# Second layer with three projection banks, a head's softmax beside the output projection, and reordered loads

## What is computed

```python
def dilated_mixer(h, w_in, w_out):
    q, k, v, z = jnp.split(h @ w_in, 4, axis=-1)            # 16 heads of 128
    q = rotary(q, pos) * (B_HEAD_DIM ** -0.5)
    k = rotary(k, pos)
    for window, dilation in B_CONFIGS:                      # (128,1), (512,4), (2048,16)
        o_g, lse_g = _dilated_band_attention(q, k, v, window, dilation)
    alpha = jax.nn.softmax(jnp.stack(lses), axis=0)
    o = jnp.einsum('gbsh,gbshd->bshd', alpha, jnp.stack(outs))
    return (o * jax.nn.silu(z)) @ w_out

def reference(x, norm_g, final_g, ...):
    h = x
    for layer in range(DEPTH):                              # DEPTH = 2
        u = rmsnorm(h, norm_g[layer])
        h = h + mixer(u, w_in, w_out)                       # dsa_mixer, then dilated_mixer
    return rmsnorm(h, final_g)
```

## Time and profile before

| | |
|---|---|
| median of 3 runs | 967.16 us (965.05 to 967.76) |
| the profiled execution | 967.73 us; its span, first to last instruction, 964.9 us |
| PE busy | 936.3 us, 97% of the span, 4603 matmuls |
| DVE / POOL / ACT busy | 647.5 (67%) / 563.4 (58%) / 443.2 us (46%) |
| mean granted clock of the matmul engine | 0.994 of full |
| chain that ended last | PE 76%, DVE 17%, issue 3%, POOL 2%, DMA 1%, ACT 1% |
| HBM read | 78.52 MB, 84 GB/s over the span |

### The profile page before, as it was taken

One profiled execution on the slowest core, in us unless ns is written; L12 is line 12 of the kernel. 1 busy time (PEld: TensorE's weight loads), 2 busy tenths in 40 slices (PEclk: granted clock), 3 DMA queues, 4 the chain that ended last, 5 costly groups with the idle time before them and its releaser, 6 DMA issues.

```text
span 964.9 us, 12633 instructions
## 1 busy us (share of the span) xinstructions
PE 936.3 (97%) x4603; PEld 790.9 (82%) x4603; DVE 647.5 (67%) x1241; ACT 443.2 (46%) x770; POOL 563.4 (58%) x395
## 2 busy tenths in 40 slices
PE   6999999999999999999899999999999999999996
PEld 5898888888888888878688888888888888878886
DVE  4798798665665644467776776666677677654456
ACT  6565323544544632355344554454445445442323
POOL 2875444555555444476666666667676676654445
PEclk9999999999999999999999999999999999999998
DMA  8422223121121122312222222221222212213212
GB/s 301 151 88 83 93 88 107 47 66 44 45 66 44 44 88 91 106 66 88 69 84 81 73 88 88 66 88 66 88 80 73 87 66 88 88 44 96 101 66 87
DMA packets 25133, 81.43 MB, mean 84 GB/s; under 512 B 2928, under 2 KB 5232, under 8 KB 25072
## 3 DMA queue, kind: packets, MB, share of 16 engines
q1 hardware_dynamic: 23920, 79.57, 24.8%
q10 hardware_dynamic: 1152, 1.06, 0.3%
HBM read 78.52 MB, written 2.10 MB: 84 GB/s over the span
## 4 chain that ended last, share of the span: by engine, by line
PE 76%; DVE 17%; issue 3%; POOL 2%; DMA 1%; ACT 1%; SPq 0%; POOLq 0%; DVEq 0%; ACTq 0%
PE ps L312 14%; PE ps L314 13%; PE ps L313 13%; DVE bias_a L1007 11%; PE ps L422 6%; PE ps L421 6%; PE ps L420 6%; DVE by_sin L927 2%; PE ps L371 2%; PE ps L372 2%; PE ps L370 2%; PE ps L385 2%; DMA w_raw<-weights 1%; PE ps L412 1%; PE ps L411 1%
## 5 line engine op out<-in xcount | busy, mean ns | idle before, releaser
L1205 POOL TENSOR_TENSOR w_lo<-w_raw,w_hi 128x1024 fp32r<-128x1024 f32 x137 | 338.2, 2469 | 301.9 <-ACT w_hi L581 301.3
L312 PE MATMUL ps<-u_hi,w_hi 128*128 128x512 f32 (+1 forms) x856 | 337.2, 394 | 17.6 <-DVE u_lo L870 8.3
L314 PE MATMUL ps<-u_hi,w_lo 128*128 128x512 f32 (+1 forms) x856 | 331.7, 388 | 0.0
L313 PE MATMUL ps<-u_lo,w_hi 128*128 128x512 f32 (+1 forms) x856 | 331.3, 387 | 0.0
L581 ACT ACTIVATE w_hi<-w_raw 128x1024 fp32r<-128x1024 f32 x138 | 146.0, 1058 | 217.4 <-PE ps L314 112.2
L312 PEld LDWEIGHTS ps<-u_hi,w_hi 128*128 128x128 f32 x856 | 161.6, 189 | 54.4 <-DVE by_cos L928 13.4
L314 PEld LDWEIGHTS ps<-u_hi,w_lo 128*128 128x128 f32 x856 | 161.4, 189 | 31.8
L313 PEld LDWEIGHTS ps<-u_lo,w_hi 128*128 128x128 f32 x856 | 161.8, 189 | 29.7 <-issue 0.5
L1007 DVE STREAM_TRANSPOSE bias_a<-probs 32x320 f32<-32x320 f32 x240 | 120.6, 502 | 4.7 <-POOL probs L1248 1.6
L1248 POOL TENSOR_SCALAR probs<-probs,inv_den 128x512 f32<-128x512 f32 (+3 forms) x128 | 66.1, 540 | 48.6 <-DVE inv_den L996 48.6
L660 ACT ACTIVATE probs<-neg_s,neg_max 128x512 f32<-128x512 f32 (+3 forms) x128 | 70.6, 554 | 23.4 <-DVE neg_max L989 23.2
(11 more groups left out here) (149 smaller groups left out, 1541.4 us busy)
## 6 DMA issues: line engine op xcount, KB each, us to landing
w_raw<-weights SPq DMA_DIRECT2D x138, 512.0 KB, 3.2
gated<-x_rows SPq DMA_DIRECT2D x4, 512.0 KB, 8.0
h<-x_turned SPq DMA_DIRECT2D x7, 256.0 KB, 7.4
outT<-h SPq DMA_DIRECT2D x10, 128.0 KB, 1.9
outT<-h ACTq DMA_DIRECT2D x6, 128.0 KB, 2.2
w_raw<-weights SPq DMA_DIRECT2D x2, 256.0 KB, 5.4
table<-rope_tables SPq DMA_DIRECT2D x2, 256.0 KB, 7.0
table<-rope_tables SPq DMA_DIRECT2D x1, 512.0 KB, 6.4
```

The lines of the kernel that those rows point to most:

```text
L312: pe.matmul(out, w_hi[:, g % SLOTS, blk], u_hi[:, k, tokens], start=(at == 0), stop=False)
L313: pe.matmul(out, w_hi[:, g % SLOTS, blk], u_lo[:, k, tokens], start=False, stop=False)
L314: last = pe.matmul(out, w_lo[:, g % SLOTS, blk], u_hi[:, k, tokens], start=False, stop=(at == KT - 1))
L1205: pool.tensor_tensor(w_lo[:, g % SLOTS, :], w_raw[:, g % 2, :], w_hi[:, g % SLOTS, :].bitcast(F32), ALU.subtract).then_inc(w_lo_ready, 1)
```

## The change

- `BANK`: the projections of the second layer go through banks 0, 1 and 7 in turn.
- `head_b`: head hd's gate is projected in the same iteration, behind its V. VectorE reads the gate's bank behind V's, no longer ahead of the transposes. On ScalarE the silu and the load back to Exp move behind the rounding of K and of the next tile, directly ahead of `v_part`. ScalarE and POOL split their four weight tiles one tile later in the list. In iteration 15 only two steps of the gate's projection stand ahead of the output of head 14, then `last_head`.
- `last_head` (PE): scores, turn of V, six steps of the gate's projection; then blocks 2, 3 and 4 of row 0 of the output projection, `turn_probs`, block 1, `output`. `out_projection(1, 0)` leaves these four blocks out. On the other engines the last head's work is the second branch of iteration 15; there is no iteration 16.
- First layer: the first two steps of query 3 are taken ahead of `turn_probs(0)`.
- Start: SP issues tiles 2 and 3 ahead of the half table, then the identity, then all rows; ScalarE squares the rows behind the rounding of tile 3.

The diff, with little context:

```diff
@@ -51,7 +51,7 @@
-BANK[N_B + 3] = 7
+BANK[N_B:] = [(0, 1, 7)[i % 3] for i in range(4 * HEADS)]
@@ -71,6 +71,8 @@
 S_BANK, T_BANK = 2, 5
+FREE_BLOCKS = (2, 3, 4)
+BEGUN_BLOCKS = FREE_BLOCKS + (1,)
@@ -244,15 +246,13 @@
                 sp.dma_start(h[:, m, :], xT[m * P:(m + 1) * P, :]).then_inc(x_landed[m], 16)
+            load_tile(2)
+            load_tile(3)
             sp.dma_start(table[0:P // 2, 2:4, :], rope_tables[0:P // 2, 2:4, :]).then_inc(key_table_landed, 16)
-            load_rows(0)
-            load_tile(2)
-            load_rows(1)
-            load_tile(3)
-            load_rows(2)
-            load_rows(3)
             sp.dma_start(ident[:, :], ident_in).then_inc(ident_landed, 16)
+            for i in range(QB):
+                load_rows(i)
@@ -428,6 +428,8 @@
                 for m in M_ORDER:
+                    if layer and t == 0 and m in BEGUN_BLOCKS:
+                        continue
@@ -464,13 +466,16 @@
                 if query:
-                    project(G_Q[hd], range(0, KT // 2))
+                    project(G_Q[hd], range(2 if hd == 3 else 0, KT // 2))
                     output(hd - 3)
                     project(G_Q[hd], range(KT // 2, end))
+                if hd == 2:
+                    project(G_Q[hd + 1], range(0, 2))
@@ -486,32 +491,31 @@
             def head_b(hd):
-                new, last_new = hd < HEADS, hd == HEADS - 1
                 n, tile = HEADS + hd - 1, G_B + 4 * hd
-                if new:
-                    scores(n, 0, R_B + 2 * hd - 1)
-                    if hd > 1:
-                        project(tile - 1)
-                    project(tile)
-                    project(tile + 1)
-                    project(tile + 2, range(0, 5 if last_new else KT))
-                    if hd == 1:
-                        pe.wait_ge(bank_read[7], 1)
-                    output_by_parts(n)
-                else:
-                    project(tile - 1, range(0, 2))
-                    turn_v(tile - 2)
-                    project(tile - 1, range(2, 6))
-                    pe.wait_ge(v_lo_ready, HEADS + 1)
-                    turn_probs(n)
-                    project(tile - 1, range(6, KT))
-                    output(n)
-                if last_new:
-                    scores(n + 1, 0, R_B + 2 * hd + 1)
-                    project(tile + 2, range(5, KT))
-                if new and not last_new:
+                scores(n, 0, R_B + 2 * hd - 1)
+                for g in range(tile, tile + 3):
+                    project(g)
+                project(tile + 3, range(0, 2 if hd == HEADS - 1 else KT))
+                output_by_parts(n)
+                if hd < HEADS - 1:
                     turn_v(tile + 2)
+            def last_head():
+                n, tile = 2 * HEADS - 1, G_OUT[1]
+                scores(n, 0, R_B + 2 * HEADS - 1)
+                turn_v(tile - 2)
+                project(tile - 1, range(2, KT))
+                wait_for_head(1, 0)
+                for m in FREE_BLOCKS:
+                    out_block(1, 0, m, ALL, True, False)
+                pe.wait_ge(v_lo_ready, HEADS + 1)
+                pe.wait_ge(bank_read[7], BANK.count(7))
+                turn_probs(n)
+                pe.wait_ge(bank_read[1], BANK.count(1))
+                out_block(1, 0, 1, ALL, True, False)
+                output(n)
@@ -560,8 +564,9 @@
             first_head_b()
-            for hd in range(1, HEADS + 1):
+            for hd in range(1, HEADS):
                 head_b(hd)
+            last_head()
@@ -695,32 +700,26 @@
             def head_b(hd):
-                new, attend, last_new = hd < HEADS, hd > 0, hd == HEADS - 1
                 n, tile, r = HEADS + hd - 1, G_B + 4 * hd, R_B + 2 * hd
-                if attend:
-                    split_w(tile + 1)
-                if not new:
-                    v_part(hd)
-                    split_o(1, 0)
-                if attend and new:
+                if hd:
                     split_w(tile + 2)
-                    silu(n, hd - 1, tile - 1)
+                    split_w(tile + 3)
+                    turned_hi(n)
+                rope_hi(r, q_hi[:, 0, :])
+                split_w(tile + 4)
+                rope_hi(r + 1, k_hi[:, :])
+                split_w(tile + 5)
+                if hd < HEADS - 1:
+                    silu(n + 1, hd, tile + 3)
                     act.preload_act_table(ACT.Exp)
-                    split_w(tile + 3)
-                if attend and new:
-                    turned_hi(n)
-                if not new:
-                    probs_hi(n)
-                    silu(n, hd - 1, tile - 1)
-                if new:
-                    rope_hi(r, q_hi[:, 0, :])
-                    split_w(tile + 4)
-                    rope_hi(r + 1, k_hi[:, :])
-                if last_new:
+                    v_part(hd + 1)
+                else:
                     exps(n + 1)
-                elif new:
                     v_part(hd + 1)
+                    split_o(1, 0)
+                    silu(n + 1, hd, tile + 3)
+                    probs_hi(n + 1)
@@ -749,11 +748,9 @@
             split_w(2)
-            square_rows(0)
-            square_rows(1)
             split_w(3)
-            square_rows(2)
-            square_rows(3)
+            for i in range(QB):
+                square_rows(i)
@@ -807,7 +804,7 @@
             act.preload_act_table(ACT.Exp)
-            for hd in range(HEADS + 1):
+            for hd in range(HEADS):
@@ -1047,32 +1044,28 @@
             def head_b(hd):
-                new, attend, last_new = hd < HEADS, hd > 0, hd == HEADS - 1
                 n, tile, r = HEADS + hd - 1, G_B + 4 * hd, R_B + 2 * hd
-                if attend and new:
+                if hd:
                     invert(n)
-                    scale_gate(n, tile - 1)
                     rope(r, tile)
-                if not new:
-                    split_o(1, 0)
-                    probs_lo(n)
-                if not new:
-                    scale_gate(n, tile - 1)
-                if new:
-                    rope(r + 1, tile + 1)
-                if last_new:
+                rope(r + 1, tile + 1)
+                scale_values(tile + 2)
+                if hd < HEADS - 1:
+                    scale_gate(n + 1, tile + 3)
+                    if hd:
+                        gate(n, hd - 1)
+                    v_part(hd + 1)
+                else:
                     mask_scores(n + 1, bias_b, lambda i: SEQ - (i + 1) * P)
-                if new:
-                    scale_values(tile + 2)
-                if last_new:
                     invert(n + 1)
-                if attend and not last_new:
-                    gate(n, hd - 1)
-                if new:
                     v_part(hd + 1)
+                    split_o(1, 0)
+                    scale_gate(n + 1, tile + 3)
+                    probs_lo(n + 1)
+                    gate(n + 1, hd)
@@ -1267,22 +1260,18 @@
             def head_b(hd):
-                new, attend = hd < HEADS, hd > 0
                 n, tile, r = HEADS + hd - 1, G_B + 4 * hd, R_B + 2 * hd
-                if attend and new:
-                    split_w(tile + 1)
+                if hd:
                     split_w(tile + 2)
-                elif attend:
-                    normalise(n)
-                    split_w(tile + 1)
-                if new:
-                    if attend:
-                        split_w(tile + 3)
-                        turned_lo(n)
-                    rope_lo(r, q_hi[:, 0, :], q_lo[:, 0, :])
-                    split_w(tile + 4)
-                    rope_lo(r + 1, k_hi[:, :], k_lo[:, :])
+                    split_w(tile + 3)
+                    turned_lo(n)
+                rope_lo(r, q_hi[:, 0, :], q_lo[:, 0, :])
+                split_w(tile + 4)
+                rope_lo(r + 1, k_hi[:, :], k_lo[:, :])
+                split_w(tile + 5)
+                if hd == HEADS - 1:
+                    normalise(n + 1)
```

## The result

| us | before | changed |
|---|---|---|
| median, 6 runs each, side by side | 966.65 (964.45 to 967.76) | 960.94 (958.88 to 964.36) |
| ratio | | 0.9948 [0.9923, 0.9974] |
| median in a later comparison, 14 and 9 runs | 966.41 | 962.65, ratio 0.9960 [0.9945, 0.9974] |
| profiled execution | 967.73 | 959.58 |
| its span | 964.9 | 957.8 |

The change makes the kernel faster, by 5.7 us in the first comparison and 3.8 in the second. The forecast was 10.7. The 15 times of the changed kernel don't lie about one value: five are between 958.88 and 960.99, ten between 962.30 and 964.36. The profiled execution is one of the lower five, so the profile alone would mislead: it shows 8.15 us gained. One of the upper ten (963.03) has a span of only 959.4 us; the other nine have 960.5 to 962.5, and the lower five 957.1 to 959.2.

A forecast was written before the change was run, and what follows sets the result against it. The matmul engine was taken as the bound, busy 936.3 of 964.9 us. Terms -1.7 - 0.9 - 4.8 - 6.0 + 2.4 = -11.0 took 967.7 to 956.7 profiled; forecast 956.5, range 952.5 to 961.5.

The forecast's parts named there:

- Ordinary heads: 14 second-layer heads: most of the 0.45 us lost per head before V's projection goes, -6.0 us (bounds -6.5 and -2.8).
- The ring: Second layer, chain from one head's mask to the next: 26.24 us against the matmul engine's 26.25, nothing to spare.
- rival (a): Second layer: the silu load waits for `z_f`, heads take 26.9 us, 965 in all; chance 0.12 shared with 26.5 us heads.
- (e): Rival, second layer: a 1.38 us drain at each table switch makes heads 29.0 us, near 995 in all; chance 0.01.
- Last head: Head 31 to the end: longer `k_lo` wait, 3.2 to 4.0 us, and short new waits, +2.4 us (bounds +0.9 and +4.2).
- First head: Second layer's first head: the 4.39 us `by_cos` wait shrinks to 1.3, full clock assumed, -4.8 us (bounds -3.0 and -6.3).
- rival (b): Other second-layer heads: POOL's weight split beats K's rotation on VectorE, heads take 28.2 us, 983 in all; chance 0.03.
- a head that starts late stays late, but loses nothing more: Second layer: as mask-to-mask chain and matmul period fit exactly, 0 to 0.3 us of old loss remains in all.
- The term of -0.4: Iteration 2 of the second layer: its even share, -0.43 us, of the -6.0 forecast for 14 heads.
- First layer: First layer: two steps of query 3 cover the 1.0 us wait for `probs`, -0.9 us (bounds -0.4 and -1.4).
- Loads: Start: tile 2 lands near 15.8 us, its 2.1 us wait shrinks to 0.4, -1.7 us (bounds 0 and -2.2).
- Rival (c): Start and first layer: the loads bring nothing and the first layer gives its gain back, 959 us; chance 0.10.

The follow-up runs named there:

- experiment 4: The changed kernel with a second silu, 0.54 us of ScalarE work, in each head of iterations 0 to 14: 968.97 us, ratio 1.0033.
- Experiment 2: The changed kernel with K's low part ahead of the weight split on GpSimd in the second layer: 958.75 us, ratio 0.9910 to the kernel before.
- experiment 3: The changed kernel with silu and the two table loads moved to the next iteration, behind ScalarE's second weight split: 955.82 us, ratio 0.9884 to the kernel before.
- experiment 8: The changed kernel with GpSimd's first sum of squares between the layers waiting for VectorE's second low part of u: 963.53 us, 12 runs.
- Experiment 9: The changed kernel with GpSimd's split of weight tile 5 waiting until VectorE has scaled the two index tables: 960.9 us, 6 runs.
- experiment 7: The changed kernel with the old order of the first loads and of ScalarE's splits beside them: 960.23 us, ratio 0.9936 to the kernel before.
- experiments 6: The changed kernel without the four output projection blocks begun early, done in their ordinary place instead: 962.65 us, 9 runs.
- experiment 1: The kernel before with only the new order of loads (and ScalarE's sums of squares behind the split of tile 3): 968.9 us, ratio 1.0012.
- experiment 5: The changed kernel with silu and table loads in the next iteration and K's low part ahead of the weight split: 954.63 us, ratio 0.9878 to the kernel before.
- experiment 11: The kernel of experiment 5, new loads kept, with GpSimd's split of tile 5 behind the two table scalings: 954.0 us, ratio 0.9873 to the kernel before.
- 10: The kernel of experiment 5 with the old order of the first loads: 953.22 us, ratio 0.9868 to the kernel before.

## Why the prediction was right or wrong

**Ordinary heads: right.** The forecast had 0.43 us each and 26.2 to 26.3 from head to head; it is 0.48 and 26.23. The ring was put at 26.24, the trace has 26.19 from mask to mask, and experiment 4 shows that it binds. The silu load doesn't wait for `z_f`, so rival (a) is out, and so is (e): 0.02 us lie between silu and the Exp load that follows (450.02 behind 449.37 + 0.63). The drain of 1.38 us that the Trainium skill, *ScalarE: Activation LUTs*, section *What ACT_TABLE_LOAD costs*, adds to a switch is in none of these rows; the measured rows decide.

**Last head: right in the main.** 3.3 us of wait for `k_lo` where 3.2 to 4.0 was forecast, and 0.2 for `o_lo` behind the last output, 0.5 with the restart where 0.7 was. Between the turn and its use the output's first product comes 0.21 us late (0.44 us behind the one before it, 857.33 to 857.77, instead of 0.23), as forecast. One wait was not forecast: 0.34 us for `pT_lo` at 840.31, before the output of head 14, which now has only two steps of the gate's projection ahead of it. In all +2.45 against +1.97. Experiment 2 shows what the wait for `k_lo` is made of: putting `k_lo` ahead of one 2.79 us split took 1.4 us from it.

**First head: the right mechanism.** The wait was forecast at 1.3 and is 1.17, at full clock as I took it. The loss of the iteration is 2.04 instead of 1.45, as `k_lo` is 0.32 late at its end and each restart costs some tenths. Answers to the earlier trace rows agree with the steps: the mask at 452.55 (453.3), `by_cos` ends at 468.41 (469.2), both sooner by about the 0.73 us by which the head itself begins sooner.

**Iteration 2: the step that failed in the second layer.** This is a wait that the sum put at nothing. The working took the 2.71 us rotation of iteration 1 as a mark of that head and set rival (b) only for the fourteen others. It never put it into the ring. In the old order nothing that the matmul engine waited for hung on it; in the new one the next mask does, since `k_hi`, the tables and `v_hi` follow it on ScalarE. The words "a head that starts late stays late, but loses nothing more" hold from iteration 3 on. They don't hold for the delay that enters in iteration 1, 2.0 us that the matmul engine had not yet waited for: it pays them at 497 us as a second `by_cos` wait of 1.42 us. Experiment 2 takes 1.5 of the 1.74 us away by removing the collision, experiment 3 all of it by removing what hangs on it. The term of -0.4 came out as +1.23.

**First layer: mis-sized.** -0.59 against -0.9. The wait for `probs` fell from 1.0 to 0.4, not to nothing. It is within the bounds.

**Loads: the step that failed most.** The forecast said that rows landing late would matter only if later than the spread allows. Tile 2 did as forecast: its wait fell to 0.2. SyncE and ScalarE show what became late instead (issue of tile 5; squares of the last row block and the root of their sums; the split of tile 5):

```profile
13.87 1.88 SPq L239 DMA_DIRECT2D gated<-x_rows  x4
...
22.02 0.33 SPq L236 DMA_DIRECT2D w_raw<-weights  x1
```

```profile
23.93 1.06 ACT L620 ACTIVATE gated<-gated 128x1024 f32<-128x1024 f32 x1
...
25.17 0.30 ACT L624 ACTIVATE root_turned<-row_sums,eps 128x4 f32<-128x4 f32 x1
...
29.67 1.06 ACT L586 ACTIVATE w_hi<-w_raw 128x1024 fp32r<-128x1024 f32 x1 [1.56 <-DMA w_raw<-weights]
```

Tile 5 is issued 2.4 us sooner than before (22.02 for 24.44), lands 1.9 us later (29.65 for 27.75) and so is split 1.9 us later (29.67 for 27.77), behind the backlog of four row blocks and three tables. The root comes at 25.17 instead of 23.92. So GpSimd's split of tile 5 moved from 28.91 to 30.81, and VectorE's table scalings from 31.77 to 29.75: two things that had been 2.9 us apart the right way round now meet. Even where VectorE wins, the gain is used up on the way: of 1.95 us at the spread (26.64 for 28.59) 0.76 are left at the first index scores (41.18 for 41.94) and 0.14 at the first `k`, `q` scores. GpSimd's low parts of the index keys are no sooner (33.43 for 33.23), and VectorE is 98% busy from 30 to 90 us in both kernels. Where GpSimd wins, 2.5 to 3.6 us are lost. By their times two thirds of the runs go that way (10 of 15 of the changed kernel, 9 of 12 in experiment 8); only the profiled ones show it directly. Experiment 9 sets that order and takes the second group away; experiment 7 does the same by the old loads. Rival (c) had this term at zero; that it could be positive was missing, and the bounds of 0 and -2.2 left it out.

**The sum at the medians.** The gain is 5.7 us in the first comparison, 3.8 in the second, and 6.5 without the new loads (experiment 7): on the median these don't give, they take. Of the 5.0 us between the gain that was forecast (10.7) and the first comparison, 1.7 are iteration 2, 0.5 iteration 1, 0.5 the last head and 0.3 the first layer; the ordinary heads give 0.7 back. The other 2.7 are the loads, as far as the spread of the runs lets one say. (The forecast's own sum, 956.7 less the 0.6 by which the profiled run lay above the median, is 956.1 and not 956.5, a slip of 0.4.) The direction was right and the range of 952.5 to 961.5 held 960.94, but not the 962.65 of the second comparison.

## What to carry to other kernels

When a change moves work of VectorE and GpSimd against each other, write down for each pair which one comes first and by how many tenths, in every head and not in the typical one: here 0.2 us either way was worth 2 us, and a long instruction that was harmless in the old order (2.71 us in the earlier trace rows) cost 1.5 us once something hung on it. Before crediting an earlier load, follow what it pushes back up to the next engine that has no slack. And look at the spread of the times, not at one profile: two groups 3 us apart were the sign of an arrival that falls either way.

## What the runs showed of the hardware

The moment at which a transfer lands differs from run to run, here by enough to decide who comes first on VectorE and GpSimd. In the two profiles of the changed kernel tile 5 landed at 29.65 and at 28.42 us, and the same two scalings took 1.28 and 4.57. (In experiments 6 and 8 it landed at 30.00 and 29.74, and VectorE was the late one, with the scalings at 30.59 and 30.69; there they took 3.51 and 3.48.) The loser waits for the other's instruction to end, and VectorE, once behind, meets the next one too. In the 4.57 us the first scaling takes 2.87 and ends 0.55 us behind GpSimd's split of tile 5 (29.58 to 32.32); the second takes 1.77 and ends 0.55 us behind GpSimd's next instruction (32.46 to 34.02). The Trainium skill, *SBUF — State Buffer*, section *SBUF: two separate sides*, has the shared port held for a whole instruction; these ends agree with it. The same at the boundary of the layers at 418 to 420 us: twelve of fourteen profiles pass it in 99.7 to 99.9 us, two in 103.2 and 104.2. Part of that is the clock, which is at half for a while in these two alone: it is granted 0.83 from 430 to 440 us in experiment 1 and 0.68 in experiment 4. In experiment 1 GpSimd's sum of squares starts 0.04 us behind VectorE's low part:

```profile
419.60 1.88 DVE L867 SCALAR_TENSOR_TENSOR u_lo<-h,gain,u_hi 128x512 fp32r<-128x512 f32 x1
```

```profile
419.64 1.29 POOL L1210 TENSOR_TENSOR square_sum<-gated 128x512 f32<-128x512 f32 x1 [1.24 <-ACT gated L591]
```

VectorE takes 1.88 us there. In the changed kernel's profile the pair starts at 418.22 and 418.27, just as close and in the same order, and VectorE takes 0.74 while GpSimd takes 1.86. So the recorded starts don't tell who goes first when they are 0.04 us apart, and what tips it stays open: experiment 8 kept GpSimd away from that low part, and only one profile of it was taken.

The clock of the matmul engine fell to half (1.2 instead of 2.4 GHz) after waits of the same length in some runs and not in others. Before the last scores `k_lo` was waited for 1.8 us in experiments 5 and 11; the windows of 840 to 845 us show it, experiment 5 first (busy time and instructions of the engines, then the granted clock, the share of the transfers and GB/s):

```profile
840.00:845.00 5.00, 3.21 (x23) 2.90 (x22) 3.03 (x10) 2.32 (x5) 3.97 (x3) 1.00 0.00 0
```

```profile
840.00:845.00 5.00, 4.73 (x20) 4.30 (x21) 1.91 (x8) 2.01 (x7) 4.89 (x3) 0.66 0.27 93
```

From the last scores to the last pair of sums of squares experiment 5 takes 103.93 us and experiment 11 takes 105.33: 1.4 us for the clock alone. All eight profiles with a wait of 3.2 us or more there have half clock behind it. Of the six with 1.8 or 1.9 us four have it (the kernel before, experiments 1, 2 and 11) and two don't (5 and 10): there the length of the wait didn't foretell it.
